# Dealing an expert's token positions over runs of eight slots in a mixture-of-experts decoder layer

## The reference

```
s = sigmoid(h @ w_router); sb = s + b_router              # h: (576, 1024)
...  # four of eight groups are kept, then the top 8 experts of a token
wts = s[eidx] / sum(s[eidx]) * 2.5
for each expert e, over the tokens that chose it:
    xb = h[tok]                                           # gather rows of 4 KB
    hb = silu(xb @ we_g[e]) * (xb @ we_u[e])              # 1024 -> 256
    acc[tok] += wt * (hb @ we_d[e])                       # 256 -> 1024
y = acc + shared_expert(h)
```

## Time and profile before

| | |
|---|---|
| median of 3 runs | 1125.97 us (1125.91 to 1126.48) |
| the profiled execution, its own time | 1126.64 us |
| its span, first to last instruction | 1124.8 us |
| TensorE busy | 1094.1 us (97%) |
| VectorE, ScalarE, GpSimd busy | 462.7, 236.4, 135.3 us |
| moved by DMA | 337.16 MB, 300 GB/s over the span |

### The profile page before, as it was taken

The page is one execution under the profiler, slowest core; times in us unless marked ns, Lnnn a source line. Parts: engine busy times, 40 slices in busy tenths (PEclk is TensorE's granted clock), DMA queues, the critical chain, the costliest instruction groups (busy, mean ns, idle before and its releaser), DMA issues.

```text
span 1124.8 us, 16922 instructions
## 1 busy us (share of the span) xinstructions
PE 1094.1 (97%) x6443; PEld 575.1 (51%) x6443; DVE 462.7 (41%) x1286; ACT 236.4 (21%) x516; POOL 135.3 (12%) x163
## 2 busy tenths in 40 slices
PE   6999999999999999999999999999999999999896
PEld 3456677777877545754343443443444444343232
DVE  2218541565456645843274233233232232331157
ACT  4131241222133123211111111111111111111111
POOL 0210000000020010121112112111111121121100
PEclk9999999999999999999999999999999999999999
DMA  9857622021170273899999999999999999999598
GB/s 370 326 207 295 227 79 75 1 85 51 62 266 7 103 255 120 311 365 426 423 425 426 424 417 425 425 416 396 421 409 384 426 399 400 417 391 370 209 412 344
DMA packets 51655, 337.16 MB, mean 300 GB/s; under 512 B 9637, under 2 KB 14089, under 8 KB 30831
## 3 DMA queue, kind: packets, MB, share of 16 engines
q1 hardware_dynamic: 33710, 287.32, 63.0%
q0 software_dynamic: 17856, 48.68, 11.8%
HBM read 311.30 MB, written 37.24 MB: 310 GB/s over the span
## 4 chain that ended last, share of the span: by engine, by line
PE 91%; DMA 4%; DVE 2%; ACT 1%; issue 1%; SPq 0%; DVEq 0%; POOLq 0%; ACTq 0%
PE bank L1561 30%; PE bank L1584 15%; PE bank L1257 10%; PE bank L1276 5%; PE bank L1549 4%; DMA mem<-expert_out_rows 3%; PE bank L1375 3%; PE bank L1376 3%; PE bank L1170 3%; PE bank L1493 3%; PE bank L1254 3%; PE bank L1145 1%; PE bank L1572 1%; PE bank L1340 1%; PE bank L1154 1%; PE bank L1128 1%
## 5 line engine op out<-in xcount | busy, mean ns | idle before, releaser
L1561 PE MATMUL bank<-mem 128*32 128x512 f32 (+2 forms) x1488 | 304.5, 594 | 0.6 <-DVE mem L2247 0.6
L1561 PEld LDWEIGHTS bank<-mem 128*32 128x32 f32 (+2 forms) x1488 | 100.6, 126 | 166.0 <-issue 166.0
L1584 PE MATMUL bank<-mem 128*32 128x512 f32 (+2 forms) x744 | 157.0, 596 | 0.1
L2247 DVE COPY mem<-bank 128x512 f32<-128x512 f32 x48 | 33.2, 691 | 283.3 <-PE bank L1549 283.3
L1257 PE MATMUL bank<-hT,mem 128*128 128x288 f32 x512 | 133.3, 410 | 1.0 <-ACT mem L935 1.0
L1257 PEld LDWEIGHTS bank<-hT,mem 128*128 128x128 f32 x512 | 93.9, 190 | 25.7 <-issue 2.4
L1561 PE MATMUL bank<-x_sb,mem 128*32 128x512 f32 (+2 forms) x416 | 99.3, 594 | 0.0
L1065 ACT ACTIVATE mem<-bank 128x256 f32<-128x256 f32 x48 | 18.4, 384 | 313.0 <-PE bank L1572 312.8
L1584 PEld LDWEIGHTS bank<-mem 128*32 128x32 f32 (+2 forms) x744 | 48.7, 126 | 61.4 <-issue 60.6
L2262 DVE COPY hT<-bank 128x512 f32<-128x512 f32 x48 | 33.2, 691 | 85.7 <-PE bank L1584 85.6
L790 POOL DMA_INDIRECT mem<-ffn_in_rows,idxg x32 | 32.9, 1028 | 264.5 <-DVE idxs L2243 211.0
(11 more groups left out here) (400 smaller groups left out, 1281.2 us busy)
## 6 DMA issues: line engine op xcount, KB each, us to landing
mem<-k_w_exp SPq DMA_DIRECT2D x51, 2048.0 KB, 23.3
mem<-in_w_exp_down SPq DMA_DIRECT2D x51, 1024.0 KB, 22.7
x_sb<-k_w_exp SPq DMA_DIRECT2D x13, 2048.0 KB, 21.4
mem<-k_w_ada SPq DMA_DIRECT2D x8, 2048.0 KB, 9.0
mem<-k_w_in SPq DMA_DIRECT2D x7, 2048.0 KB, 9.7
hT<-in_w_exp_down SPq DMA_DIRECT2D x13, 1024.0 KB, 25.4
mem<-expert_out_rows SPq DMA_DIRECT2D x6, 2048.0 KB, 16.5
mem<-k_w_head SPq DMA_DIRECT2D x4, 2048.0 KB, 18.4
```

What stands on the lines that cost most here:

```text
L1561: i = mm(bank[sl, :], xT[:, j % 2, c * BLK + sl.start:c * BLK + sl.stop], wview(r)[0][:, c, :], start=c == 0, stop=c == KC - 1)
L1584: i = mm(ps[4 + hf][sl, :], hhT[:, k * BLK + sl.start:k * BLK + sl.stop], wview(r)[1][:, k, hf * 512:(hf + 1) * 512], start=k == 0, stop=k ...
```

## The change

A table `deal` is made beside the other constants, with four parts, one for each width k = 1 to 4 quarters. Part k holds the numbers 0 to 32k-1 of `iota` in transposed order: read in runs of eight slots, run e holds the positions e, 4k+e, 2*4k+e, and so on. `slots_of` compares with this table in place of `iota`. The token with position p of an expert (less what earlier blocks hold) therefore goes to slot 8*(p mod 4k) + p div 4k: neighbours in position stand eight slots apart, every run of eight partitions gets its share of the tokens, and the empty slots are the last ones of each run, where before they were the last ones of the expert.

```diff
+DR = 8
...
+        deal = sb("deal", [P, 10 * QS], BF16)
...
+        def dealt(k):
+
+            return deal[:, k * (k - 1) // 2 * QS:k * (k + 1) // 2 * QS]
...
             dve.memset(oneb, 1.0)
+            for k in range(1, P // QS + 1):
+                cp(dealt(k).rearrange("p (e r) -> p e r", r=DR), iota[:, 0:k * QS].rearrange("p (r e) -> p e r", r=DR))
             cp(trib, cst["tri"][:, :])
...
                 w = pm.shape[-1]
-                return stt(pm, p.to_broadcast([P, NT, w]), off, iota[:, 0:w].unsqueeze(1).to_broadcast([P, NT, w]),
+                return stt(pm, p.to_broadcast([P, NT, w]), off, dealt(w // QS).unsqueeze(1).to_broadcast([P, NT, w]),
                            ALU.add, ALU.is_equal)
```

## The result

Four runs gave a median of 1135.53 us (1134.15 to 1138.05), the kernel before 1125.94 beside it: a ratio of 1.009, 95% interval 1.007 to 1.0111. The change costs 9.6 us. The profiled execution took 1134.15 us and was the fastest of the four. I had forecast 1126.8 with a range up to 1129.5 and a chance of 0.21 for slower: wrong.

The account below looks back on a forecast made before the run. TensorE was taken to set the time, with weights just fast enough. 1126.64 us profiled plus 0.3 (last expert's weights) and 0.3 (last scatter) gave 1127.2, 1126.6 as median; leaning upward, the forecast was 1126.8 us, range 1125.0 to 1129.5.

Parts of the forecast that it names:

- What bounds the kernel, and which transfers change: Expert stage: TensorE sets the time, weights come just fast enough; only the split of gather and scatter rows over engines changes.
- The split in runs of four, 32 apart: Gathers and scatters: engine = 8*(partition >> 6) + ((partition >> 2) & 7), so the change fills even engines and thins odd ones.
- A split by partitions 8n to 8n+7: Rival on row split: engines levelled after all, fullest engine's rows fall from 376 to 298, 1125.5 us; chance 0.1.
- Terms 1, 2 and 6: Four casts (0, bounds 0 and 0.95 us), bfloat16 comparisons (0), first gather (0.16 us on the engine, counted 0).
- Term 5: Last scatter: 6 rows on the fullest engine become 8; +0.3 us taken, bounds -1.5 and +0.7.
- The block of twice the length at half the level: Sign expected in the last scatter's DMA view: 8 engines busy, about twice as long, in place of a short full block.
- Term 3: Weights through most of the expert stage: tightest margin 0.6 us, landing 0.3 us earlier or the same; 0, bound about +1 us.
- the slow rival: Expert stage: full even engines, also carrying instruction fetches, make weights late in many places, 3 to 20 us; chance 0.15.
- Term 4: Last expert's weights: nine more rows, 1.47 us, overrun the 1.24 us margin by 0.23; +0.3 us taken, bounds 0 and 1.5.

## Why the prediction was wrong, point by point

- **What bounds the kernel, and which transfers change:** right. TensorE sets the time, the weights come just fast enough, and the change only moves rows between engines (the runs with the old order, with levelled engines and with half rows).
- **The split in runs of four, 32 apart:** borne out as far as it was used. The order meant to level runs of eight makes the engines uneven, and the one made for runs of four has no wait. A split by partitions 8n to 8n+7 is ruled out, since the change would then have had no late weights. The Trainium skill, "DMA: Bandwidth & Descriptors", section The descriptor swizzle, gives this split, and the traces agree: with eight, four or one engine full by this split, eight, four or one completion of a load come late.
- **Terms 1, 2 and 6** (casts, comparisons, first gather): right, 0. The casts used 0.35 of the 1.22 us of cover.
- **Term 5, the last scatter:** +0.07 us by the chain, where I took +0.3. The block of twice the length at half the level, forecast as a sign, is there.
- **Term 3 failed, and it is the step that decides.** I wrote that the fullest engine's rows were 352 before and 350 after, "so it lands 0.3 us earlier or the same", with a bound of about +1 us. That takes the engine with the most rows for the slowest engine. It holds only if the engines are alike but for the rows. They are not: at one row count, engine 0 costs 3.9 us and engines 4 and 6 cost 8.4 and 11.6. With about the same rows on the fullest engine, the three loads that count landed 3.3, 6.9 and 6.9 us later than before. Before, the old order happened to give the most rows to engines 0, 1 and 2 and few to 10 and 14 (284 and 189), whose other work lay hidden behind the rows of engine 0. The change lifted them to 375 and 373. I had the thought, in the slow rival, and priced it at 1130 to 1146 us, where the result fell; but I made it hang on instruction fetches that all sit on one even engine ("spread over many it adds less than 2 us"), and gave it 0.15. The mechanism was right in "had few rows before and is now as full as the fullest", wrong in "even": the odd set costs the same. The times of the steps speak for the fetches as the cause, and against my price for them when spread. A landing tells nothing of an engine that is never the last one; the sixteen completion events of the same trace do, and I had not read them.
- **Term 4 failed with it.** I took the last expert, with a margin of 1.24 us, as the only one at risk. Waits came at 783.88, 963.66 and 1038.04 us, and none at the last expert. Its load took 20.4 us in place of 15.0, not the 1.47 us more that nine rows give, and was in time only because the wait and the slow matmuls before it had moved its use back by 4 us, on top of the margin. Of the three loads that were waited for, two had a recorded landing before, with margins of 1.5 and 5.6 us. The bound of 1 us on the delay left them out. The third, at 1038.04, has no landing in the views of before, and I took it for safe.
- **A price that I had no term for:** the clock. Of 7.2 us in the profiled execution, 1.7 are what the matmuls after the longest wait lost at a granted clock of 0.51 and 0.64.

What is open: whether the other work of engines 4, 6, 10 and 14 is the instruction fetches, as the times say, or something in step with them; no run here took the fetches away. The other ten engines were not tried singly.

## What to carry to other kernels

Where many DMA engines share one load, it lands with the slowest engine. A mean share of 0.97 to 1.01 does not say which that is, and counting bytes per engine does not either as long as their other work is unknown; the completion events of a load do. If TensorE has no wait on a transfer, levelling that transfer cannot help (here it brought the weights 7.5 us earlier and the kernel nothing), while an order that fills the engines anew can expose what was hidden. Look for the margins of all loads first, and treat a missing landing as a margin of zero. A helper that "deals over groups of eight" must be matched to the real split of partitions over engines: here an order dealt over groups of four costs nothing (tried as a constant table, not with the helper).

## What the runs showed of the hardware that was not expected

- The DMA engines are not interchangeable in this kernel: at 380 or 384 rows, a single full engine costs from 3.9 us (engine 0) to 12.8 us (engine 14), with the same total of bytes. Four of the six tried fall back by about 2 us at a time, at the times of instruction fetches eight apart.
- After a wait of 2.31 us the granted clock of TensorE was 0.51 and 0.64 over the next four microseconds, which made that wait 1.7 us dearer; after one of 1.78 us it stayed at 1.00. The length of the wait alone does not decide it: in the run with engine 15 full a wait of 2.96 us ended at 1036.94, and the clock was 1.00 from 1036 to 1042 us.
- The casts that stand beside GpSimd's two memsets end when these do: 2.29 us for the old cast before, 2.89 us for four casts together after, and then 0.21 us for the old one.
